# Two vector-engine steps of attention's older units put ahead of the newest unit's maximum

## The reference

```
def windowed_gqa(q, k, v, sink):
    ...
    m = jnp.maximum(jnp.max(s, axis=-1, keepdims=True), sk)
    p = jnp.exp(s - m)
    denom = jnp.sum(p, axis=-1, keepdims=True) + jnp.exp(sk - m)
    o = jnp.einsum('bnhgqk,bnkhd->bnqhgd', (p / denom).astype(v.dtype), vw)
...
def blocked_attention(q, k, v, scale):
    ...
        sc = jnp.einsum('bqhgd,bkhd->bhgqk', qblk, k).astype(jnp.float32) * scale
        p = jax.nn.softmax(sc, axis=-1).astype(v.dtype)
        return jnp.einsum('bhgqk,bkhd->bqhgd', p, v)
```

## Time and profile before

| | us |
|---|---|
| median of three runs | 3573.54 (3572.11 to 3580.22) |
| profiled execution, its own time | 3572.58 |
| its span | 3570.7 |
| PE busy | 3522.3 (99%) |
| DVE busy | 1430.0 (40%) |
| ACT busy | 1353.5 (38%) |
| POOL busy | 1950.8 (55%) |
| chain that ended last, share of PE | 91% |

### The profile page before, as it was taken

The page is one execution under the profiler, slowest core; times in us unless marked ns, Lnnn a source line. Parts: engine busy times, 40 slices in busy tenths (PEclk is TensorE's granted clock), DMA queues, the critical chain, the costliest instruction groups (busy, mean ns, idle before and its releaser), DMA issues.

```text
span 3570.7 us, 45976 instructions
## 1 busy us (share of the span) xinstructions
PE 3522.3 (99%) x18316; PEld 2858.7 (80%) x18316; DVE 1430.0 (40%) x2294; ACT 1353.5 (38%) x2200; POOL 1950.8 (55%) x2418
## 2 busy tenths in 40 slices
PE   9999999999999999999999999999999999999999
PEld 8888868888888888748888886788888877888887
DVE  4221766231423148676322266325111475244022
ACT  4322354322332235574332336434233345334231
POOL 6555545555565547744655457545555555546553
PEclk9999999999999999999999999999999999999999
DMA  4333303333233332202333320132333210323332
GB/s 136 95 92 97 100 18 99 97 94 97 92 96 96 92 99 95 63 1 82 106 99 93 104 79 19 58 96 89 95 95 95 96 56 13 95 83 101 95 95 76
DMA packets 87717, 301.53 MB, mean 84 GB/s; under 512 B 9936, under 2 KB 14544, under 8 KB 87120
## 3 DMA queue, kind: packets, MB, share of 16 engines
q1 hardware_dynamic: 85392, 296.50, 26.9%
q10 hardware_dynamic: 2112, 2.10, 0.2%
HBM read 296.46 MB, written 2.10 MB: 84 GB/s over the span
## 4 chain that ended last, share of the span: by engine, by line
PE 91%; DVE 6%; ACT 1%; DMA 1%; issue 1%; POOL 0%; SPq 0%; ACTq 0%; DVEq 0%; POOLq 0%
PE bank L306 25%; PE bank L308 25%; PE bank L307 25%; PE bank L869 2%; PE bank L846 2%; PE scores L831 2%; DVE sqsum L507 2%; DVE xl L497 1%; DVE x L435 1%; DVE tmp L428 1%; PE bank L1928 1%; PE bank L1930 1%; PE bank L1929 1%; PE bank L1315 1%; PE bank L1317 1%; PE bank L1351 1%
## 5 line engine op out<-in xcount | busy, mean ns | idle before, releaser
L295 POOL TENSOR_TENSOR w_lo<-w_raw,w_hi 128x256 fp32r<-128x256 f32 x2210 | 1680.4, 793 | 1425.4 <-ACT w_hi L283 1424.8
L283 ACT ACTIVATE w_hi<-w_raw 128x1024 fp32r<-128x1024 f32 (+2 forms) x567 | 586.0, 1037 | 1220.9 <-DMA w_raw<-in_ffn_up 374.5
L306 PE MATMUL bank<-xh,w_hi 128*128 128x512 f32 x2544 | 998.4, 392 | 1.2 <-DVE o_g L1570 1.2
L308 PE MATMUL bank<-xh,w_lo 128*128 128x512 f32 x2544 | 990.0, 389 | 0.0
L307 PE MATMUL bank<-xl,w_hi 128*128 128x512 f32 x2544 | 989.7, 389 | 0.0
L306 PEld LDWEIGHTS bank<-xh,w_hi 128*128 128x128 f32 x2544 | 478.4, 188 | 103.3 <-issue 3.1
L307 PEld LDWEIGHTS bank<-xl,w_hi 128*128 128x128 f32 x2544 | 478.6, 188 | 100.1 <-issue 2.4
L308 PEld LDWEIGHTS bank<-xh,w_lo 128*128 128x128 f32 x2544 | 478.2, 188 | 99.5
L306 PE MATMUL bank<-hh,w_hi 128*128 128x512 f32 (+1 forms) x1336 | 502.0, 376 | 0.0
L307 PE MATMUL bank<-hl,w_hi 128*128 128x512 f32 (+1 forms) x1336 | 500.9, 375 | 0.0
L308 PE MATMUL bank<-hh,w_lo 128*128 128x512 f32 (+1 forms) x1336 | 500.9, 375 | 0.0
(11 more groups left out here) (402 smaller groups left out, 4194.2 us busy)
## 6 DMA issues: line engine op xcount, KB each, us to landing
w_raw<-in_ffn_up SPq DMA_DIRECT2D x176, 512.0 KB, 3.5
w_raw<-in_ffn_down SPq DMA_DIRECT2D x64, 512.0 KB, 3.5
w_raw<-in_b_ffn_up SPq DMA_DIRECT2D x64, 512.0 KB, 3.5
w_raw<-in_b_ffn_down SPq DMA_DIRECT2D x64, 512.0 KB, 3.5
w_raw<-in_b_gates SPq DMA_DIRECT2D x48, 512.0 KB, 3.5
w_raw<-in_od_in SPq DMA_DIRECT2D x33, 512.0 KB, 3.3
w_raw<-in_ffn_down SPq DMA_DIRECT2D x32, 384.0 KB, 3.1
w_raw<-in_b_in SPq DMA_DIRECT2D x24, 512.0 KB, 3.3
```

The costliest lines, as they stand in the source:

```text
L283: act.activation(w_hi[:, g % RING, 0:widths[g]], w_raw[:, g % RING, 0:widths[g]], ACT.Copy)\
L295: ins = pool.tensor_tensor(w_lo[:, slot, part], w_raw[:, slot, part], w_hi[:, slot, part].bitcast(F32), ALU.subtract)
L306: pe.matmul(out, wh, hi, start=first, stop=False)
L308: return pe.matmul(out, wl, hi, start=False, stop=last)
```

## The change

In `attend_dve` the blocks for the reciprocal of unit s-1 and for the copy of unit s-3 stand ahead of the block for the maximum of unit s. Nothing else differs: the same instructions with the same waits, and the other engines' lists are the same. Lines in this function get other numbers: the maximum is L898 (was L885), the small operations L900, L902, L904 and L907 (were L887, L889, L891, L894), the reciprocal L885 with L884 ahead of it in `even` (were L901, L900), the copy L891 (was L907).

```diff
             for s in range(n + BEHIND + 3):
                 if s in early:
                     early[s]()
+                if 0 <= s - 1 < n:
+                    u, g = units[s - 1], c.units + s - 1
+                    r = red[:, g % 4, :]
+                    dve.wait_ge(probs_ready, g + 1)
+                    if u["nsink"] is not None:
+                        ch.link(dve.tensor_tensor(r[:, 4:6], r[:, 4:6], r[:, 6:8], ALU.add))
+                    dve.reciprocal(r[:, 8:10], r[:, 4:6]).then_inc(sums_inverted, 1)
+                if 0 <= s - BEHIND < n:
+                    u, g = units[s - BEHIND], c.units + s - BEHIND
+                    dve.wait_ge(turned_b, g + 1)
+                    if g >= 2:
+                        dve.wait_ge(attended, g - 1)
+                    dve.tensor_copy(turned[g % 2][:, 1, 0:u["keys"]], bank[TURNED + 1][:, 0:u["keys"]]).then_inc(copied_b, 1)
                 if s < n:
...
                         dve.tensor_scalar(r[:, 2:4], r[:, 0:2], -u["scale"], None, ALU.mult).then_inc(rowmax_ready, 1)
-                if 0 <= s - 1 < n:
...
-                if 0 <= s - BEHIND < n:
...
                 e = s - BEHIND - 2
```

## The result

The changed kernel takes 3647.5 us (median of 3 runs, 3647.46 to 3647.57) against 3573.5 before: ratio 1.0203, with an interval of 1.0189 to 1.0217. It is slower by 74 us; the forecast was 3639, slower by 66. The profiled execution has a span of 3645.6 us, 74.9 more than before.

The account below looks back on a forecast made before the run. TensorE, busy 99% of the span, was taken to bound the kernel. Losses of 20.3 + 21.4 (full attentions) + 24.4 (windowed) = 66.1 us on the profiled 3572.6 gave 3638.7, so a median of 3639; range 3622 to 3662.

Parts of the forecast that it names:

- The circle of exponential and maximum: All attentions: reciprocal waits for its unit's exponential, so exponential and maximum alternate; grouped loop 3.85 against 2.93 us; chance 89%.
- a windowed round: Windowed attention: four units take 13.3 us against 9.0 before; the stretch 76.0 against 51.8, 24.4 us lost in all.
- The stall in the small operation: VectorE's small operation blocked until GpSimd's scaling ends, in nearly every loop; makes the loss 66 us rather than 59.
- The bound without it: Lower bound with GpSimd's scaling out of the way: grouped loop 3.77, windowed round 12.7, loss some 59 us, time 3632.
- The start of a full attention: First units of each full attention: maximum 0 to maximum 3 takes 5.8 + 7.7 + 0.9 = 14.4 us.
- The latent part: Paired latent units, maximum 17 to 31 of each full attention: 7 pairs of 7.79 us, 54.5 us.
- The sum: Losses of both full attentions and the windowed one: 20.3 + 21.4 + 24.4 = 66.1 us, giving 3639.
- The rival of the falling clock: TensorE's new gap in each loop lowers its clock; for a quarter of 88 units 44 us more, 3683; chance 7%.
- a clock that leaves 1.00 in attention: Sign named as proving the forecast wrong: TensorE's granted clock in attention departing from its full level, 1.00.
- TensorE stays the bound: Rival: the exponential-to-exponential loop fits under 2.93 us, so nothing is lost; 3568 or 3573; chance 4%.
- the handovers of 0.1: Mis-sizing case: three engine handovers of 0.03 to 0.05 us could be 0.1 each, 17 us more over 85 loops.
- The latent slack of 0.2: Latent pairs: TensorE finishes only 0.2 us before the copy asks; if broken by 0.3, 16 pairs lose 5 us more.

Follow-up runs that it names:

- e5: Changed kernel with two one-column activations added behind side 0's exponential in each unit; 3665.4 us (1.0259).
- e6: Kernel before the change with two one-column activations added behind side 0's exponential in each unit; 3578.6 us (1.0011).
- e3: Changed kernel with GpSimd's scaling of the probabilities cut to one column of each side, the rest left unscaled; 3638.9 us (1.0179).
- e8: Changed kernel with 8, 7 and 10 idle matmul calls filling TensorE's longest gaps in the full attentions and the windowed attention; 3642.9 us (1.019).
- e2: Changed kernel with the reciprocal put back behind the small operation, only the copy staying ahead of the maximum; 3597.6 us (1.0061).
- e1: Changed kernel with the copy put back behind the small operation, only the reciprocal staying ahead of the maximum; 3641.9 us (1.0189).
- e4: Changed kernel with 17, 15 and 20 idle matmul calls in TensorE's longest gaps, a fill twice too long; 3652.9 us (1.022).

## Why the prediction was right, point by point

- *The circle of exponential and maximum* is shown. Its loops came out as worked out: grouped 3.85 (3.85 forecast), latent 4.18 + 3.63 = 7.81 (4.13 + 3.66 = 7.79), the joint behind a grouped unit 4.36 + 3.63 (8.0), a windowed round 13.3 (13.3), the windowed length 76.2 (76.0). e5 and e6 show that the path goes through ScalarE.
- *The stall in the small operation*: shown, and its size roughly: forecast 7, measured 9 to 11. The bound without it was 59 lost (3632); e3 lost 65 (3638.9), 62.8 of it in the three lengths. Its loop (3.77 forecast, 3.79) and its round (12.7, 12.7) were right; what the bound lacked is the start of the full attentions, still long in e3 (5.9 and 6.9 from maximum 2 to 3).
- *The start of a full attention* is the term that was mis-sized: 14.4 forecast from maximum 0 to 3, 16.6 and 16.5 measured. I took the value projection between maxima 2 and 3 as hidden and TensorE's clock as full. It ran at the lower level; with the gaps filled (e8) maximum 0 to 3 is 14.4 and 14.0. This is 2.2 + 2.1.
- *The latent part*: 7 x 7.79 = 54.5 forecast, 56.2 measured, by the two pairs of 8.59 in each stretch. I had looked at GpSimd's scaling in front of the small operation and not at its other work, the rests of the roundings. This is 1.7 twice.
- *The sum*: the last two points are 4.3 + 3.4 = 7.7, with 0.2 in the windowed part 7.9 of the 8.1 by which the lengths exceed the forecast (74.0 less 65.9); the last 0.9 of the span's 74.9 lies outside, where I had 0.2. The low clock behind the windowed units (2.5) is part of the 3.6 us that this stretch is longer. The errors in the lengths all have one sign, so the number came out well for the size of its main term and not by errors that cancel. (3638.7 and 0.96 are 3639.7; I wrote 3639.)
- *The rival of the falling clock*: wrong in its place, right in its mechanism. The trains of short gaps kept 1.00, and no 44 us were lost. But I had named a clock that leaves 1.00 in attention as a sign against me, and it did, in three places for 7.2 us (e8) and in a fourth, at 472 to 478, for some 0.3. So by that sign the forecast was in part wrong. The earlier trace rows had shown a fall behind just such a wait; I priced it as a whole rival and not as a term where the new gaps are long.
- *TensorE stays the bound* and *the handovers of 0.1*: excluded by the loops (3.85 measured, with TensorE idle for 0.7 to 0.85 of it).
- *The latent slack of 0.2*, the copy waiting for TensorE: it held in the kernel after (VectorE waits in the reciprocal, not in the copy). e2 shows the same circle standing by itself, at 10.7 of its 24 us; I had called it a bound from above and then expected next to nothing from it in e2, which was wrong.

## What to carry over

In an engine's list that runs in order, ask of each instruction with a wait what stands behind it: a reciprocal of 0.17 us that waits for the newest exponential made two overlapping engines alternate and cost 0.92 us in every grouped unit, with not one instruction added. Work the new circle out by its pieces from rows and compare it with the pace of the engine that bounds now; that came within 1% a loop. Then look for what is not periodic, the starts, the ends and the places where a helper engine does something else, since the rest of the error was there.

## What was not expected of the hardware

- Taking 0.7 us of work out of the grouped circle gave nothing there, since the wait of a small VectorE operation for GpSimd's scaling filled its place (e1: small operation 0.82 instead of 0.22, loop 3.85 in both).
- Gaps of 0.7 to 0.85 us in each 3.85 never lowered TensorE's clock. Waits of 1.8 to 2.4 us were followed by 0.50 in some places and by 1.00 in others, also at the same place of two programs (e8 and the kernel after) and of the two full attentions of one (e4).
- Filling a gap with matmuls that nothing reads kept the clock up and bought 2.2 to 2.5 us a place, when the fill was no longer than the gap; twice as long, it lost more than it kept (maximum 2 to 3 took 7.54 and 7.63 us, against 7.05 and 6.71 without a fill).
